# Residual rows inside the combining product, with the tiles' rows loaded by halves and quarters of the partitions

## The reference, cut to what matters

```python
def post_norm(x, y, w, b):
    return layer_norm(DEEPNORM_ALPHA * x + y, w, b)
...
    y = hier_moe(tokens, router_wg[l], router_bg[l], router_we[l], router_be[l], moe_w1[l], moe_w3[l], moe_w2[l])
    h_lat = post_norm(h_lat, m[5] * y[:B * S].reshape(B, S, D), ln_w[l, 1], ln_b[l, 1])
```

## Time and profile before

| | us |
|---|---|
| median of 3 runs | 2293.1 |
| the runs | 2295.09, 2291.28, 2293.1 |
| the profiled execution's own time | 2294.9 |
| its span, first to last instruction | 2293.0 |
| TensorE busy | 2173.0 (95%) |
| VectorE busy | 809.1 (35%) |
| ScalarE busy | 402.9 (18%) |
| GpSimd busy | 351.0 (15%) |
| mean granted TensorE clock | 0.981 |
| DMA, mean over the span | 250 GB/s |

### The profile page before, as it was taken

The page is one execution under the profiler, slowest core; times in us unless marked ns, Lnnn a source line. Parts: engine busy times, 40 slices in busy tenths (PEclk is TensorE's granted clock), DMA queues, the critical chain, the costliest instruction groups (busy, mean ns, idle before and its releaser), DMA issues. The chain is left out here.

```text
span 2293.0 us, 27961 instructions
## 1 busy us (share of the span) xinstructions
PE 2173.0 (95%) x10576; PEld 1049.7 (46%) x10576; DVE 809.1 (35%) x1711; ACT 402.9 (18%) x862; POOL 351.0 (15%) x382
## 2 busy tenths in 40 slices
PE   6999999899999999999997999999998999999996
PEld 3547545777555343334432444444553343334431
DVE  2694213556626311111111633434455111111114
ACT  2301042554211111011111410100111100110112
POOL 0000012222131100201000423221320010201003
PEclk8999999999999999999999999999999999999998
DMA  9892000001336999999998411114327999999997
GB/s 388 330 370 81 1 0 1 2 2 38 130 112 231 373 419 419 419 413 419 410 419 353 177 37 55 37 55 159 146 111 271 416 419 419 404 419 419 415 395 300
DMA packets 135816, 572.50 MB, mean 250 GB/s; under 512 B 25049, under 2 KB 38521, under 8 KB 93690
## 3 DMA queue, kind: packets, MB, share of 16 engines
q1 hardware_dynamic: 123002, 537.04, 59.1%
q0 software_dynamic: 12672, 33.57, 3.8%
HBM read 548.52 MB, written 34.62 MB: 254 GB/s over the span
## 5 line engine op out<-in xcount | busy, mean ns | idle before, releaser
L1287 PE MATMUL bank<-bigA,bigB 128*32 128x512 f32 (+2 forms) x1888 | 481.3, 603 | 13.7 <-DMA bigA<-in_moe_w 9.0
L867 PE MATMUL bank<-bigC,bigB 128*128 128x512 f32 (+3 forms) x768 | 293.7, 538 | 0.0
L1287 PEld LDWEIGHTS bank<-bigA,bigB 128*32 128x32 f32 (+2 forms) x1888 | 158.0, 133 | 237.7 <-issue 230.0
L1311 PE MATMUL bank<-bigA,bigB 128*32 128x512 f32 (+2 forms) x912 | 242.4, 594 | 3.6 <-DVE bigB L2237 3.1
L867 PEld LDWEIGHTS bank<-bigC,bigB 128*128 128x128 f32 x768 | 143.4, 194 | 128.4 <-issue 119.8
L1287 PE MATMUL bank<-bigC,bigB 128*32 128x512 f32 (+2 forms) x560 | 171.4, 593 | 0.0
L1363 PE MATMUL bank<-bigB,bigA 128*128 128x512 f32 x384 | 170.7, 592 | 0.0
L1477 ACT ACTIVATE bigB<-bank,small 128x128 f32<-128x128 f32 x280 | 104.6, 460 | 371.4 <-PE bank L818 371.2
L2561 POOL DMA_INDIRECT y_rows<-bigB,ints x42 | 42.4, 1009 | 810.1 <-DVE bigB L2242 810.1
L2233 DVE TENSOR_TENSOR bigB<-bigB,bank 128x512 f32<-128x512 f32 x42 | 28.9, 688 | 306.9 <-PE bank L1287 306.9
L2242 DVE TENSOR_TENSOR bigB<-bank,gate 128x512 f32<-128x512 f32 x84 | 54.1, 686 | 233.5 <-PE bank L1311 233.5
(11 more groups left out here) (351 smaller groups left out, 2608.5 us busy)
## 6 DMA issues: line engine op xcount, KB each, us to landing
bigA<-in_moe_w SPq DMA_DIRECT2D x250, 1024.0 KB, 24.8
bigC<-in_moe_w SPq DMA_DIRECT2D x80, 1024.0 KB, 23.9
bigA<-in_ada_w SPq DMA_DIRECT2D x40, 1024.0 KB, 6.8
misc<-in_moe_w SPq DMA_DIRECT2D x36, 1024.0 KB, 25.5
lnwb<-in_moe_w SPq DMA_DIRECT2D x18, 1024.0 KB, 25.9
bigA<-y_rows SPq DMA_DIRECT2D x14, 1024.0 KB, 13.6
bigA<-in_w_in_odd SPq DMA_DIRECT2D x12, 1024.0 KB, 5.3
bigA<-in_ada_w SPq DMA_DIRECT2D x4, 2048.0 KB, 13.7
```

The source lines that it names most:

```text
L867: last = mm(bank(n % 3)[:, 0:w], uT[:, k, t * P:(t + 1) * P], wring[:, g % 2, k, at_:at_ + w], start=(k == 0), stop=(k == KC - 1))
L1287: last = mm(bank(m)[at_:at_ + w, :], xT[:, j, KC // 2 * h + k, at_:at_ + w], w13_at(SLOT_OF[m, h, q][0], k), start=(h == 0 and k == 0), st ...
L1311: last = mm(bank(6 + n)[at_:at_ + w, :], gT[:, 2 * h + k, at_:at_ + w], w2_at(SLOT_OF[2, h, q][0], k)[:, n * 512:(n + 1) * 512], start=(h ...
```

## The change

A tile's tokens are taken in four groups of 32. Group g = 2h + q has its 64 expert rows in half h of the tile, in partitions 64q to 64q+63, and its 32 residual rows now in the other partitions of the same half-tile: 64+32h to 95+32h for q = 0, 32h to 32h+31 for q = 1. The matrix `share[:, t, g, :]` is [128, 32] and has weights in 64 of its rows, alpha in 32, and zeros in 32. So one product per group and half of the width does both jobs, and the four groups' products are issued side by side. `residual_part` and its products are gone. Each half-tile now needs separate copies for q = 0 and q = 1, so each tile takes 2 MB of SBUF, and the loads change:

- pair rows: 18 transfers in place of 9, each to 64 partitions (0 to 63 for q = 0, 64 to 127 for q = 1) in turn, 512 KB each (tile 0: four of 256 KB);
- residual rows: 28 transfers in place of 4, each to 32 partitions, 128 KB each (256 KB for tiles 5 and 6 together); those of tiles 2, 1, 4, 7 where all were loaded before, those of tiles 0, 5, 6, 3 after it, behind waits for more slots (13, 10, 1 and 6 are last read by the last step's output products).

`share` gets one more GpSimd operation (adding the permuted `alpha_i`, 128x1024), behind a wait for the 16 it has. `alpha_i` is made by two VectorE instructions in place of one.

```diff
-ROW_SLOTS = (9, 11, 14, 15)
-ROW_LOADS = [int(n <= 8 or n in ROW_SLOTS) for n in range(SLOTS)]
+TILE_SLOTS = ((12, 13), (14, 15), (9, 11), (10, 1), (16, 17), (4, 0), (5, 6), (7, 3))
+ROW_LOADS = [{12: 6, 13: 2, 14: 6, 9: 6, 10: 6, 16: 6, 4: 6, 5: 2, 7: 6}.get(n, 0) for n in range(SLOTS)]
...
+        tile_runs = [[hh[:, q:4:2], hh[:, 4 + q:8:2], blocks[:, 12 + q:16:2, :], (blocks[:, 16:19:2, :], blocks[:, 17:24:6, :])[q],
+                      consts_run[:, q:4:2, :], blocks[:, q:4:2, :], blocks[:, 4 + q:8:2, :], blocks[:, 8 + q:22 + q:13, :]] for q in range(2)]
+
+        def row_part(h, q):
+            return slice(32 * h, 32 * h + 32) if q else slice(64 + 32 * h, 96 + 32 * h)
...
-                for n, slot in enumerate(ROW_SLOTS):
-                    last_use(slot)
-                    dst = blocks[:, 12 + 2 * n:14 + 2 * n, :] if n < 2 else hh[:, 2 * n:2 * n + 2]
-                    load(dst, h_dram[l][2 * n * P:2 * (n + 1) * P, :].rearrange("(t p) n -> p t n", p=P), f"w_in_{slot}")
+                def tile_rows(t, n):
+
+                    for slot in [slot for i in range(n) for slot in TILE_SLOTS[t + i]]:
+                        last_use(slot)
+                    for h in range(2):
+                        for q in range(2):
+                            rows = h_dram[l][t * P:(t + n) * P, :].rearrange("(t g i) n -> i t g n", g=4, i=32)[:, :, 2 * h + q, :]
+                            if n == 1:
+                                dst, rows = tile_runs[q][t][row_part(h, q), h, :], rows.squeeze(1)
+                            else:
+                                dst = blocks[row_part(h, q), 2 * h + q:8:4, :]
+                            load(dst, rows, f"w_in_{TILE_SLOTS[t][0]}")
+
+                for t in (2, 1, 4, 7):
+                    tile_rows(t, 1)
...
+                tile_rows(0, 1)
+                tile_rows(5, 2)
+                tile_rows(3, 1)
...
-                    if t == 0:
-                        load(pair[0][:, :, 0:512], rows[:, :, 0:512], "w_in_0")
-                        load(pair[0][:, :, 512:], rows[:, :, 512:], "w_in_8")
-                    else:
-                        load(pair[t], rows, f"w_in_{t}")
+                    for n in range(2 if t == 0 else 1):
+                        cols = (slice(0, 512), slice(512, D))[n] if t == 0 else slice(0, D)
+                        for q in range(2):
+                            half = slice(64 * q, 64 * q + 64)
+                            load(tile_runs[q][t][half, :, cols], rows[half, :, cols], f"w_in_{TILE_SLOTS[t][n]}")
...
-            def residual_part(l, t):
...
                 if t >= 2:
-                    residual_part(l, t)
-                pe.wait_ge(S(f"w_in_{t}"), filled(t, l, FILLS[t]))
+                    pe.wait_ge(S("nrm"), NT * (2 * l + 1) + t - 1)
+                pe.wait_ge(S(f"w_in_{TILE_SLOTS[t][0]}"), rows_filled(TILE_SLOTS[t][0], l))
...
                     for h in range(2):
-                        last = mm(bank(sum_at(t) + n)[64 * h:64 * h + 64, :], share[:, t, h, :],
-                                  pair[t][:, h, n * 512:(n + 1) * 512], start=False, stop=True, skip_group_check=True)
+                        for q in range(2):
+                            g = 2 * h + q
+                            last = mm(bank(sum_at(t) + n)[32 * g:32 * g + 32, :], share[:, t, g, :],
+                                      tile_runs[q][t][:, h, n * 512:(n + 1) * 512], start=True, stop=True, skip_group_check=True)
...
-            v.tensor_scalar(alpha_i[:, :], ident, ALPHA, None, MUL)
+            for q in range(2):
+                v.tensor_scalar(alpha_i[:, :].rearrange("p (h q i) -> p q h i", h=2, q=2)[:, q], ident[:, 64 * (1 - q):64 * (2 - q)].rearrange("p (h i) -> p h i", h=2), ALPHA, None, MUL)
...
                             for h in range(2):
-                                last = pool.tensor_scalar(share[:, t, h, :], cc("twos"), row_w[:, h, t:t + 1], None, MUL)
-                        last.then_inc(S("share_ok"), 1)
+                                G(pool.tensor_scalar(share_pair[:, t, h, :], cc("twos"), row_w[:, h, t:t + 1], None, MUL))
+                        G.wait()
+                        pool.tensor_tensor(share_all, share_all, wide(alpha_i[:, :].unsqueeze(1), [P, NT, P]), ADD).then_inc(S("share_ok"), 1)
```

More of the change, by code:

```diff
@@ L69, with rows_filled @@
     _held = sorted(_held + [(freed(_piece), _n, _slot, _piece)])
-ROW_SLOTS = (9, 11, 14, 15)
-ROW_LOADS = [int(n <= 8 or n in ROW_SLOTS) for n in range(SLOTS)]
+TILE_SLOTS = ((12, 13), (14, 15), (9, 11), (10, 1), (16, 17), (4, 0), (5, 6), (7, 3))
+ROW_LOADS = [{12: 6, 13: 2, 14: 6, 9: 6, 10: 6, 16: 6, 4: 6, 5: 2, 7: 6}.get(n, 0) for n in range(SLOTS)]
 def filled(slot, l, turn):
     return 16 * ((FILLS[slot] + ROW_LOADS[slot]) * l + turn + 1)
+def rows_filled(slot, l):
+    return 16 * (FILLS[slot] + ROW_LOADS[slot]) * (l + 1)
 WEIGHTS_OUT, WEIGHTS_IN, SHARE_STEP = 24, 30, 8
@@ L344, in program @@
         route = bigB[:, 8704:10240]
-        share = at(bigB, 8192, NT, 2, 64)
-        pair = [at(bigA, o, 2, D) for o in (17408, 19456, 21504, 0, 2048, 4096, 6144, 8192)]
-        row_at = [blocks[:, 12 + t, :] for t in range(4)] + [hh[:, t] for t in range(4, NT)]
+        share, share_pair, share_all = at(bigB, 8192, NT, 4, 32), at(bigB, 8192, NT, 2, 64), at(bigB, 8192, NT, P)
+        consts_run = misc[:, C_AT["tri0"][0]:C_AT["tri0"][0] + 4 * D].rearrange("p (b n) -> p b n", b=4)
+        tile_runs = [[hh[:, q:4:2], hh[:, 4 + q:8:2], blocks[:, 12 + q:16:2, :], (blocks[:, 16:19:2, :], blocks[:, 17:24:6, :])[q],
+                      consts_run[:, q:4:2, :], blocks[:, q:4:2, :], blocks[:, 4 + q:8:2, :], blocks[:, 8 + q:22 + q:13, :]] for q in range(2)]
+        def row_part(h, q):
+            return slice(32 * h, 32 * h + 32) if q else slice(64 + 32 * h, 96 + 32 * h)
         diag0 = lnwb[:, :].rearrange("p (j k n) -> p j k n", j=2, k=KC)
@@ L1416, in combined @@
                 if t >= 2:
-                    residual_part(l, t)
-                pe.wait_ge(S(f"w_in_{t}"), filled(t, l, FILLS[t]))
+                    pe.wait_ge(S("nrm"), NT * (2 * l + 1) + t - 1)
+                pe.wait_ge(S(f"w_in_{TILE_SLOTS[t][0]}"), rows_filled(TILE_SLOTS[t][0], l))
                 for n in range(2):
                     if t == 0 and n:
-                        pe.wait_ge(S("w_in_8"), filled(8, l, FILLS[8]))
+                        pe.wait_ge(S(f"w_in_{TILE_SLOTS[0][1]}"), rows_filled(TILE_SLOTS[0][1], l))
                     for h in range(2):
-                        last = mm(bank(sum_at(t) + n)[64 * h:64 * h + 64, :], share[:, t, h, :],
-                                  pair[t][:, h, n * 512:(n + 1) * 512], start=False, stop=True, skip_group_check=True)
+                        for q in range(2):
+                            g = 2 * h + q
+                            last = mm(bank(sum_at(t) + n)[32 * g:32 * g + 32, :], share[:, t, g, :],
+                                      tile_runs[q][t][:, h, n * 512:(n + 1) * 512], start=True, stop=True, skip_group_check=True)
                 last.then_inc(S("comb"), 1)
@@ L1438, in _ @@
             moe(0)
-            for t in range(2):
-                residual_part(0, t)
             gate_rows(2, diag1[:, 0], 2)
@@ L1461, in _ @@
             moe(1)
-            for t in range(2):
-                residual_part(1, t)
             for t in range(NT):
```

## The result

The changed kernel takes 2325.66 us (median of 4 runs, 2324.45 to 2326.08), the kernel before 2292.43 us beside it (4 runs, 2291.28 to 2295.09): ratio 1.014, 95% interval 1.0128 to 1.0152. It is 33 us slower. The profiled execution has a span of 2323.5 us, 30.5 more than before. The residual products, 34.0 us of TensorE's busy time before (line 1409), are gone. The busy time fell by less, from 2173.0 to 2150.6 us, because other products ran longer at the lower clock: the pair products take 40.2 us in place of 34.2. The time was lost in waits.

What follows compares the result with a forecast made beforehand. The prediction took the stage as TensorE-bound, with DMA a near second limit. Layer 0's +12.5 and layer 1's +11.1 us made +23.6, taking the profiled 2294.9 to 2318.5, or 2316.7 us on the median; range 2302 to 2326.

Steps and rivals of the forecast that it cites:

- Part 1: TensorE in both layers' tiles: 16 residual products per layer go, gaining 6.0 us in layer 0 and 3.0 in layer 1.
- Rival (a): Pair-row transfers to the two halves overlap at full rate, data never late: 2284 us; chance 0.15.
- Part 2: Pair rows to 64 partitions at a time: 235.5 GB/s, 35.6 us in place of 20.4, 15.2 us more per layer.
- (b): Pair-row transfers to the two halves overlap in part, some 300 GB/s: 2300 us; chance 0.10.
- Part 3: Residual rows to 32 partitions at a time: pair rows start 0 to 4.7 us later per layer, 2.4 taken.
- Part 4: GpSimd's added operation, 2.35 us, and one more VectorE instruction at the start, under 0.3 us: nothing added.
- Layer 0: Convolution weights land at 1303.5, GpSimd's fixed order delays `conv_rest(0)` by 10.6 us, lower clock adds 1.9: +12.5 us.
- Cold clock: Layer 0, `conv_rest(0)`: after TensorE idles some 5 us, its lower granted clock loses another 1.9 us.
- GpSimd would be the releaser: Layer 0, sign to look for: TensorE's wait ahead of `conv_rest(0)` is released by GpSimd.
- Layer 1: Pair rows end at 2290.7, last products at 2293.6 in place of 2282.5, the rest as before: +11.1 us.

Runs made afterwards that it cites:

- every other partition: Changed kernel with pair rows of q = 0 in even, q = 1 in odd partitions, residual rows in the other parity with step 4: 2293.91 us, ratio 1.0005.
- full-rate loads: Changed kernel with layer 1's pair and residual rows loaded whole into separate copies, its combining sum left incomplete: 2313.26 us, ratio 1.0082.
- the halves alone: Kernel before with only the pair rows' loads cut into two halves of the partitions (0 to 63, 64 to 127): 2316.19 us, ratio 1.0104.
- the quarters alone: Kernel before with only the residual rows' loads cut into 32 transfers to 32 partitions each: 2301.38 us, ratio 1.0035.
- the two single-part kernels: Kernel before with only pair rows by halves (2316.19 us), and kernel before with only residual rows by quarters (2301.38 us).
- the fill products: Changed kernel with idle products on TensorE in its waits, in layer 1's tiles and ahead of the first conv_rest: 2322.33 us, ratio 1.0124.
- fewer residual transfers: Kernel of every other partition with both groups of a run loaded by one 256 KB transfer into the same 32 partitions: 2290.59 us, ratio 0.9990.

## Why the prediction was right, and where its sizes were off

It forecast 2316.7 us, range 2302 to 2326, and slower with 0.80; measured were 2325.66 us, 0.3 us inside the upper end. The mechanism was right. The sum was too low: +23.6 us from one profiled execution to the other, where the spans differ by 30.5. The medians differ by 33.2, because the profiled execution of before (2294.9) stands 2.5 us above the median of the four runs, 2292.43, and that of after (2325.33) 0.3 below its own. All errors of size had the same sign, so that the range still holds the time is in part luck.

**Part 1, the removed products.** They went, but "9 us to be had" was too much. In layer 0, 6.0 us were said, and the version with every other partition has 4.4. In layer 1, 3.0 were said. There the step took VectorE's run of 3.5 us as the next limit and overlooked GpSimd's multiplication in it; the loop of scaling, multiplication and shift takes 3.70 us (full-rate loads, every other partition). Layer 1 could gain some 0.5 us in its tiles, and later residual rows took more than this. Rival (a)'s price fell with it: at 413 GB/s the kernel is not 9 us faster but within 0.1%.

**Part 2, pair rows.** This term was mis-sized. I took 235.5 GB/s from two pairs of `w_out_even`; eighteen transfers gave 221: 8.39 MB take 38.0 us in place of 35.6, so +17.6 per layer, not +15.2, and tiles every 4.7 us, not 4.4 to 4.5. The Trainium skill's 218 GB/s (SBUF — State Buffer, "Door 1: The DMA port swizzle"), which I left beside the sum, was the nearer figure. The two pairs were too short to average. In the first, two neighbouring microseconds read:

```profile
526.00:527.00 1.00, 1.00 (x10) 0.79 (x10) 0.96 (x8) 0.49 (x1) 0.37 (x2) 1.00 1.05 303
527.00:528.00 1.00, 0.46 (x6) 0.06 (x2) 1.00 (x11) 0.00 (x0) 0.00 (x0) 1.00 0.99 217
```

In the second the rate goes from 250 to 221. The prediction said that it does not rise where one half gives way to the other; the 303 did not bear this out, and halves that alternate faster or come from two queues do overlap in part. That rivals (a) and (b) do not hold in this kernel is shown by the halves alone on the kernel before.

**Part 3, residual rows.** The middle value, 2.4 us per layer, was too low, as the quarters alone show: some +8 us in all, 3.0 of it in layer 0. In the changed kernel three pieces can be read in layer 1: the last expert product waits 1.99 us for its weights in place of 0.89; the last scatter takes 8.04 us in place of 7.12; and first products come 8.6 us after the pair rows' issue (2267.86 to 2276.50), before 4.25. I had costed the first two at nothing.

**Part 4.** Nothing that the runs can tell, as forecast: the two single-part kernels account for the loss within their intervals.

**Layer 0.** Forecast +12.5, measured +17.5. Weights at 1305.45 (forecast 1303.5): 2.0, by the rates of parts 2 and 3. Token sums 1308.01 to 1327.88, 19.9 us in place of 17.6: 2.3, since their second tile now runs beside VectorE's token sums for tile 7 (1.1) and their third beside its multiplication and addition for the layer norm (1.2; 2.13 us at 1322.07). `conv_rest(0)` at 1329.52 (1325.3). Cold clock 2.8 in place of 1.9, as the fill products show; the idle before it is 9.00 us, where the prediction said some 5 and its own times (1303.5 + 15 to 1325.3) give 6.8. That GpSimd would be the releaser, and that it alone makes the shift, was right.

**Layer 1.** Forecast +11.1. From the last expert product to the end it is 65.8 us against 54.2, +11.6, and +1.1 for the late weights ahead of it: 12.7. The +11.6 are 0.8 until the pair rows are issued, 4.4 until their first product, 5.8 over the tiles, 0.6 at the end.

What stays open: why VectorE's shift ends with GpSimd's multiplication, why the last weights land 1.1 us later with small transfers behind them in the queue, and how large each of part 3's pieces is by itself in layer 1, where they were not separated.

## What to carry to other kernels

A layout that loads half of the partitions must be priced by which partitions, not by how many bytes: interleave the two sets (every other partition) before giving up on the idea. Before one takes work from the engine that looks like the bound, work out the loop behind it through all engines and its buffers, here 3.70 us (ScalarE, GpSimd, VectorE) against 3.78, or the gain is a wait of the same length. And when a queue gets slower, look at what stands last in it: here convolution weights behind pair rows, with an engine in fixed order behind them.

## What the runs showed of the hardware that was not expected

- A transfer of 64 partitions with a step of two runs at 413 GB/s, a contiguous one at 221, sizes and count equal.
- Contiguous halves overlap in part if they stand in two engines' queues: 299 GB/s in layer 0, 274 over 20 us of layer 1; and a little if they alternate every 256 KB: 238. The Trainium skill (SBUF — State Buffer, "Can I just issue two DMAs to hit both halves?") says that they serialise; from one queue at 512 KB the trace agrees, from two queues it does not.
- An issue for 32 spaced partitions occupies SyncE for 0.59 us (median, every other partition), one of twice the bytes for about 0.61 (fewer residual transfers), for 32 contiguous ones 0.42 (changed kernel).
- An addition of 128x512 on GpSimd takes 1.27 us alone and 2.12 to 2.13 beside VectorE's multiplication and addition of 128x1024 (the one at 1323.11 took 2.17 in place of its usual 1.22).
- VectorE's shift of 128x1 takes 0.16 us alone; where it falls into GpSimd's multiplication of 128x1024 it ends with it, after 0.48 to 1.61 us (full-rate loads in layer 1).
